# The root of a head's variance: from eleven VectorE steps to one GpSimd power instruction, for six of eight groups

## The chip, the cores and the metric

The kernel runs on one core of a Trainium2 chip. The metric is device time in microseconds (us). The kernel before takes 2485.27 us, the median of three runs (2484.48 to 2485.36). Smaller is better.

## The reference, cut to what matters

The kernel computes a two-layer decoder trunk on 256 tokens of width 2048, in float32. Layer 0 is an RWKV-7 time mix, layer 1 a block attention, and each is followed by a SwiGLU feed-forward part. The change touches one line of layer 0: the output `y` of the recurrence is normalised per token and per head of 64 columns.

```
y = _rwkv7_scan(rh, decay, kh, vh, -kk, kk * ah)        # 32 heads of 64
mu  = jnp.mean(y, axis=-1, keepdims=True)
var = jnp.mean(jnp.square(y - mu), axis=-1, keepdims=True)
yn  = ((y - mu) * lax.rsqrt(var + GN_EPS)).reshape(B, S, C) * lnx_w + lnx_b
bonus = (jnp.sum(rh * kh * r_k, axis=-1, keepdims=True) * vh).reshape(B, S, C)
return ((yn + bonus) * g) @ w_o
```

What is at issue is the factor `rsqrt(var + GN_EPS)`: 256 tokens by 32 heads, thus 8192 numbers in all.

## The kernel before, in words

All large weight products go through one scheme. SP loads a chunk of weights, ScalarE rounds it (`whi`, L1246), VectorE takes the rest (`wlo`, L1684), and TensorE does three products for each tile (L595 to L597). The recurrence lies between the projections and the output product, from about 280 to 520 us of the span.

The recurrence works on 8 groups (`GROUPS`) of 256 columns, four heads each, in 8 slots (`for s in range(GROUPS)`), one after another. Each engine has its own list of instructions in a written-out order, and semaphores join them. In slot `s` TensorE solves a triangular system for group `s` in five levels. `inner(s, l)` (L775) is a product whose result VectorE masks (L1846); `outer(s, l)` (L785) is a product whose result VectorE transposes (L1852, L1854) and ScalarE copies (L1368). Between these steps TensorE does the solution and the state of group `s - 1`, and `fill(n)` (L892, L882): pieces of a projection and of the gate, which are put there as filler. After `inner(s, 4)` TensorE runs `transposes_of(s + 1)` (L724 to L728). It waits there on `nat_done`, which GpSimd gives.

VectorE also does the normalisation of group `i = s - 2` in slot `s`, as parts of `group_norm`. Parts 0 and 1 (sum, mean and centring, L1887 to L1890) lie at the end of slot `s - 1`, then ScalarE squares (L1390). In slot `s`, part 2 (sum of squares L1893, scale and epsilon L1894) stands after `inner(s, 1)`, part 3 after `inner(s, 4)`, part 4 after `outer(s, 4)`, and part 5 (the product with the root, L1902) at the slot's end. Parts 3 and 4 are the root: two seed instructions (L1663, L1664) and three Newton steps of three (L1668 to L1670), each on 128 x 8 numbers, each waiting for the one before it. The last two groups, 6 and 7, are normalised after or at the end of the slots.

GpSimd's order in its loop over `g` from 1 to 7 is: for `g` 5 and 6 first `finish(g - 5)` and `load_w(g - 3)`; then `naturals(g)`, then `bonus(g - 2)` and `load_b(g)`. `naturals(g)` waits on `decay_done`, which ScalarE gives (L1301) in slot `g - 1`, and does five products on 128 x 512 (L507 to L511); the last gives `nat_done`. `finish(g)` multiplies the normalised group by its weight, adds the bonus and multiplies by the gate (L536 to L538); it waits on `y_normed`, which L1902 gives. `wait_aside` is a 128 x 1 instruction (L459) that carries a wait. At the start GpSimd clears `idle` (L452), waits for it, and issues three loads (L461 to L463).

Of the kernel before, what the change touches and what calls it, by code (L numbers as in the profile page):

```python
# [25 lines left out]
ALU = mybir.AluOpType  # L26
# [23 lines left out]
HD = 64  # L50
CHUNK = 64
PAIRS = D // P
GROUPS = PAIRS // 2
# [26 lines left out]
GN_EPS = 64e-5  # L80
# [74 lines left out]
def trunk(nc, x, rows, rwkv_rows, lora, w, consts, ln_rows, y):  # L155
    with ExitStack() as ctx:
        def sem(name):
            return ctx.enter_context(nc.semaphore(name))
# [10 lines left out]
        gsm = sb("gsm", [P, 5, 8])  # L169
# [4 lines left out]
        pad_ring = sb("pad_ring", [P, 176])  # L174
# [24 lines left out]
        def carve(base, at, *shape):  # L199
            n = int(np.prod(shape))  # L200
            v = base[:, at:at + n]
            if len(shape) == 1:
                return v
            names = "abcd"[:len(shape)]
            return v.rearrange(f"p ({' '.join(names)}) -> p {' '.join(names)}", **{q: n for q, n in zip(names[:-1], shape[:-1])})
# [36 lines left out]
        def mask(at, *shape):  # L242
# [11 lines left out]
        MQ = tmp("a2t", 2, 3, P)  # L254
        S = tmp("a2t", 2, 3, CHUNK)
        PC = carve(pad_ring, 0, 3, 2, 4)
        y_sq = carve(big, 32 * KB, TT, 2 * P)
        parb, parw = carve(a2t, 28 * KB, 2, 2 * P), carve(a2t, 30 * KB, 2, 2 * P)
        g2p = [tmp("rec2", 2, 2 * P) for _ in range(3)]
# [45 lines left out]
        ix_set, iz_made, iz_set, ixt_made, ixt_set, first_set, moved = (  # L305
            sem(n) for n in ("ix_set", "iz_made", "iz_set", "ixt_made", "ixt_set", "first_set", "moved"))
        y_centred, y_squared = sem("y_centred"), sem("y_squared")
        names = ("tr_made arT_set bkT_set g_made g_set av_made av_set uhw_made uhw_set "
                 "post_made s_made s_set y_made y_set")
        lq = [{n: sem(f"lane{s}_{n}") for n in names.split()} for s in range(2)]  # L310
# [139 lines left out]
        def _(pool):  # L450
            xv = x[0].rearrange("(t p) d -> p t d", p=P)
            nc.gpsimd.memset(idle[:], 0.0).then_inc(idle_set, 1)  # L452
            pool.wait_ge(idle_set, 1)

            def wait_aside(k, ready, value):

# [34 lines left out]
            def load_w(g):  # L491
                if g >= 2:
                    pool.wait_ge(zz_done, g - 1)
                load_row(parw, 3, g, parw_in)
# [7 lines left out]
            def naturals(g):  # L502

                cs = slice(g * 2 * P, (g + 1) * 2 * P)
                Pi, Pn, Pe = E[:, 0], E[:, 1], L_[:, :, cs]
                pool.wait_ge(decay_done, g + 1)
                then(5, nc.gpsimd.tensor_tensor(Pe, Pe, Pi, ALU.mult))  # L507
                nc.gpsimd.tensor_tensor(KN_[:, :, cs], KN_[:, :, cs], Pe, ALU.mult)
                nc.gpsimd.tensor_tensor(R_[:, :, cs], R_[:, :, cs], Pi, ALU.mult)
                for m in BH:  # L510
                    last = nc.gpsimd.tensor_tensor(m[:, :, cs], m[:, :, cs], Pn, ALU.mult)  # L511
                last.then_inc(nat_done, 1)
# [17 lines left out]
            def finish(g):  # L530

                yv, vv, gv = (m[:, :, g * 2 * P:(g + 1) * 2 * P] for m in (R_, KN_, L_))
                pool.wait_ge(parw_in[g % 2], 16 * (g // 2 + 1))
                wait_aside(3, gate_kept, g + 1)
                pool.wait_ge(y_normed, g + 1)
                then(4, nc.gpsimd.tensor_tensor(yv, yv, across(parw[:, g % 2]), ALU.mult))  # L536
                then(5, nc.gpsimd.tensor_tensor(yv, yv, vv, ALU.add))
                nc.gpsimd.tensor_tensor(yv, yv, gv, ALU.mult).then_inc(zz_done, 1)  # L538

            naturals(0)  # L540
            pool.wait_ge(chunk_used, PH["wo"][0])
            for g in range(2):
                load_b(g)
                load_w(g)
            for g in range(1, GROUPS):
                if g in (5, 6):
                    pool.wait_ge(y_normed, g - 3)
                    finish(g - 5)
                    load_w(g - 3)
                naturals(g)  # L550
                if g >= 2:
                    bonus(g - 2)
                    load_b(g)
            for g in range(2, 4):
                finish(g)
                load_w(g + 2)
            bonus(GROUPS - 2)
            for g in range(4, GROUPS - 2):
                finish(g)
# [672 lines left out]
        def _(act):  # L1232
# [54 lines left out]
            def decays(g):  # L1287
# [5 lines left out]
                ci = ps[:, 4].rearrange("p (t c) -> p t c", t=TT)  # L1293
                A(PC[:, g % 3].rearrange("p l c -> p (l c)"), ps[:, 6, 0:8], ACT.Exp)
                A(E[:, 0], ci, ACT.Exp)
# [355 lines left out]
        def _(dve):  # L1651
            V = nc.vector
            step = Count(dve_step)

            def then(ins):

                step.up(ins)
                dve.wait_ge(dve_step, step.now())
# [197 lines left out]
            def transitions(g, a):  # L1856
# [4 lines left out]
                V.tensor_tensor(MQ[:, a, 2, 0:CHUNK], ps[:, 5 + 2 * a, 3 * P:3 * P + CHUNK], ri[:, a, 3, 1], ALU.add)  # L1861
                V.tensor_scalar(S[:, a, 0], ps[:, 4 + 2 * a, P:P + CHUNK], PC[:, g % 3, a, 0:1], None, ALU.mult).then_inc(q["s_set"], 1)

            def state(g, c):

                at = P if c == 1 else P + CHUNK
                for a in (1, 0):
                    q = lq[a]
                    dve.wait_ge(q["s_made"], 2 * g + c)
                    V.tensor_scalar(S[:, a, c], ps[:, 4 + 2 * a + c % 2, at:at + CHUNK], PC[:, g % 3, a, c:c + 1], None,  # L1870
                                    ALU.mult).then_inc(q["s_set"], 1)

            def group_norm(i, part):

                cs = slice(i * 2 * P, (i + 1) * 2 * P)
                yv = R_[:, :, cs]

                def heads(v):
                    return v.rearrange("p t (h i) -> p t h i", i=HD)

                def per_head(v):
                    return v.rearrange("p (t h) -> p t h", t=TT).unsqueeze(3).broadcast_to([P, TT, 4, HD])

                if part == 0:
                    for q in lq:
                        dve.wait_ge(q["y_set"], i + 1)
                    then(V.tensor_reduce(gsm[:, 0].rearrange("p (t h) -> p t h", t=TT), heads(yv), AX.X, ALU.add))  # L1887
                    then(V.tensor_scalar(gsm[:, 1], gsm[:, 0], 1.0 / HD, None, ALU.mult))
                elif part == 1:
                    V.tensor_tensor(heads(yv), heads(yv), per_head(gsm[:, 1]), ALU.subtract).then_inc(y_centred, 1)  # L1890
                elif part == 2:
                    dve.wait_ge(y_squared, i + 1)
                    then(V.tensor_reduce(gsm[:, 0].rearrange("p (t h) -> p t h", t=TT), heads(y_sq), AX.X, ALU.add))  # L1893
                    then(V.tensor_scalar(gsm[:, 2], gsm[:, 0], 1.0 / HD, GN_EPS, ALU.mult, ALU.add))  # L1894
                elif part == 3:
                    rsqrt_seed(gsm[:, 3], gsm[:, 2], gsm[:, 4])
                    newton(gsm[:, 3], gsm[:, 2], gsm[:, 4])
                elif part == 4:
                    newton(gsm[:, 3], gsm[:, 2], gsm[:, 4])
                    newton(gsm[:, 3], gsm[:, 2], gsm[:, 4])  # L1900
                else:
                    V.tensor_tensor(heads(yv), heads(yv), per_head(gsm[:, 3]), ALU.mult).then_inc(y_normed, 1)  # L1902

            dve.wait_ge(chunk_used, PH["wo"][0])
# [9 lines left out]
            for s in range(GROUPS):  # L1914
                more = s + 1 < GROUPS

                def norm(part):
                    if s >= 2:
                        group_norm(s - 2, part)

                inner(s, 1)
                norm(2)
                outer(s, 1)
                inner(s, 2)
                if s:
                    transitions(s - 1, 1)
                    transitions(s - 1, 0)
                outer(s, 2)
                if s:
                    state(s - 1, 1)  # L1930
                inner(s, 3)
                if s:
                    state(s - 1, 2)
                outer(s, 3)
                inner(s, 4)
                norm(3)
                outer(s, 4)
                norm(4)
                if more:
                    masked_products(s + 1, 0)  # L1940
                inner(s, 5)
                if more:
                    first_block(s + 1, 0)
                    masked_products(s + 1, 1)
                    first_block(s + 1, 1)
                if s:
                    for part in range(2):
                        group_norm(s - 1, part)
                norm(5)
# [19 lines left out]
            def finish(g):  # L1969

                yv, vv, gv = (m[:, :, g * 2 * P:(g + 1) * 2 * P] for m in (R_, KN_, L_))
                dve.wait_ge(parw_in[g % 2], 16 * (g // 2 + 1))
                dve.wait_ge(gate_kept, g + 1)
                then(V.tensor_tensor(yv, yv, bcast_row(parw[:, g % 2]), ALU.mult))
                then(V.tensor_tensor(yv, yv, vv, ALU.add))
                V.tensor_tensor(yv, yv, gv, ALU.mult).then_inc(last_z, 1)
# [274 lines left out]
```

## Time and profile before

| | |
|---|---|
| median of 3 runs | 2485.27 us |
| lowest, highest | 2484.48, 2485.36 us |
| span of the profiled execution (first to last instruction) | 2481.7 us |
| time outside the span, against the median | 3.57 us |
| TensorE busy, instructions | 2444.9 us (99%), 15550 |
| VectorE busy | 1410.0 us (57%) |
| ScalarE busy | 1074.4 us (43%) |
| GpSimd busy | 126.0 us (5%) |
| mean granted TensorE clock | 0.998 |

The profiled execution has no time recorded for it beside its span of 2481.7 us, so the span stands for it; the 3.57 us are the difference to the median of the three timed runs. The profile names TensorE PE (its weight loads PEld), VectorE DVE, ScalarE ACT and GpSimd POOL. A row of the timeline gives the start, the time from the first start to the last end, engine, line, operation, output and input, shapes and the count of instructions merged in it. A bracket at its end gives the idle time before it and what ended that. A row of the waits gives who waited for whom, the total, the number of times and the longest. A busy TensorE is not necessarily at its peak, but here it leaves few gaps.

### The profile page before, as it was taken

How to read it: one execution, taken by the hardware profiler on the slowest of the kernel's cores; microseconds unless marked ns; L12 is line 12 of the kernel's file. 1: busy time of each engine (PE TensorE's matmuls, PEld its weight loads, DVE VectorE, ACT ScalarE, POOL GpSimd, SP SyncE). 2: the span in 40 equal slices, each digit the busy share in tenths (PEclk: the TensorE clock that was granted, in tenths of full speed). 3: DMA queues.
4: the chain of work that ended last, by engine and by line, in shares of the span. 5: the costliest groups of instructions: out<-in, count | busy, mean ns of one | idle time of the engine just before them, and what ended most of it. 6: DMA issues, size and time to landing. Idle time of an engine off the chain costs nothing.

```text
span 2481.7 us, 39434 instructions
## 1 busy us (share of the span) xinstructions
PE 2444.9 (99%) x15550; PEld 2003.2 (81%) x15550; DVE 1410.0 (57%) x1743; ACT 1074.4 (43%) x1347; POOL 126.0 (5%) x166
## 2 busy tenths in 40 slices
PE   8999999999999999999999999999999999999997
PEld 5888788877888888888887788888788888888886
DVE  6688566676744454454446544666745445454445
ACT  4454355444444444443334344453544444443332
POOL 1000235420000000000000000000000000000000
PEclk9999999999999999999999999999999999999999
DMA  7556411255666666665665565445566666666564
GB/s 233 179 195 205 136 42 38 66 208 188 196 192 188 186 193 186 188 188 193 193 195 198 195 193 188 143 167 190 170 187 192 188 186 193 186 194 221 189 194 143
DMA packets 225435, 440.87 MB, mean 178 GB/s; under 512 B 13472, under 2 KB 23744, under 8 KB 224224
## 3 DMA queue, kind: packets, MB, share of 16 engines
q1 hardware_dynamic: 221760, 417.38, 54.1%
q0 software_dynamic: 3552, 21.73, 2.6%
q8 instruction: 91, 1.49, 0.2%
q14 instruction: 32, 0.26, 0.0%
HBM read 436.96 MB, written 2.10 MB: 177 GB/s over the span
## 4 chain that ended last, share of the span: by engine, by line
PE 94%; DVE 3%; ACT 1%; issue 1%; DMA 1%; POOL 0%; DVEq 0%; ACTq 0%; SPq 0%; POOLq 0%
PE ps L595 25%; PE ps L597 25%; PE ps L596 25%; PE ps L892 3%; PE ps L1075 1%; PE ps L775 1%; PE ps L785 1%; PE ps L1103 1%; PE ps L622 1%; PE ps L624 1%; PE ps L623 1%; PE ps L882 1%; PE ps L836 1%; DVE wlo L1684 1%; PE ps L740 1%
## 5 line engine op out<-in xcount | busy, mean ns | idle before, releaser
L1246 ACT CAST whi<-raw 128x1024 fp32r<-128x1024 f32 x735 | 772.5, 1052 | 1145.9 <-PE ps L597 1080.1
L1684 DVE TENSOR_TENSOR wlo<-raw,whi 128x1024 fp32r<-128x1024 f32 x549 | 670.1, 1225 | 622.2 <-ACT whi L1246 620.3
L595 PE MATMUL ps<-whi,ahi 128*128 128x512 f32 x2172 | 851.5, 392 | 2.8 <-DVE wlo L1684 2.8
L597 PE MATMUL ps<-whi,alo 128*128 128x512 f32 x2172 | 845.6, 389 | 0.0
L596 PE MATMUL ps<-wlo,ahi 128*128 128x512 f32 x2172 | 845.1, 389 | 0.0
L595 PEld LDWEIGHTS ps<-whi,ahi 128*128 128x128 f32 x2172 | 407.8, 188 | 87.6 <-DVE wlo L1684 3.6
L597 PEld LDWEIGHTS ps<-whi,alo 128*128 128x128 f32 x2172 | 407.7, 188 | 85.5
L596 PEld LDWEIGHTS ps<-wlo,ahi 128*128 128x128 f32 x2172 | 407.9, 188 | 84.4 <-issue 1.0
L2015 DVE TENSOR_TENSOR wlo<-raw,whi 128x1024 fp32r<-128x1024 f32 x193 | 236.2, 1225 | 249.4 <-ACT whi L1246 247.4
L595 PE MATMUL ps<-whi,hThi 128*128 128x512 f32 x656 | 255.4, 389 | 0.0
L597 PE MATMUL ps<-whi,hTlo 128*128 128x512 f32 x656 | 255.2, 389 | 0.0
L596 PE MATMUL ps<-wlo,hThi 128*128 128x512 f32 x656 | 255.2, 389 | 0.0
L595 PEld LDWEIGHTS ps<-whi,hThi 128*128 128x128 f32 x656 | 123.1, 188 | 25.7
L596 PEld LDWEIGHTS ps<-wlo,hThi 128*128 128x128 f32 x656 | 123.1, 188 | 25.5
L597 PEld LDWEIGHTS ps<-whi,hTlo 128*128 128x128 f32 x656 | 123.1, 188 | 25.4
L892 PE MATMUL ps<-raw,big 128*128 128x256 f32 x256 | 67.7, 398 | 0.1
L571 POOL DMA_DIRECT2D big<-ln_rows x3 | 1.6, 537 | 1116.3 <-PE ps L624 787.1
L892 PEld LDWEIGHTS ps<-raw,big 128*128 128x128 f32 x256 | 44.8, 189 | 7.6 <-issue 0.3
L1516 ACT ACTIVATE a2t<-ps,lnT 128x128 f32<-128x128 f32 x96 | 34.2, 496 | 33.2 <-PE ps L1065 33.2
L1846 DVE TENSOR_TENSOR rec<-ps,big 128x512 f32<-128x512 f32 x40 | 27.6, 689 | 35.7 <-PE ps L775 35.7
L1693 DVE SCALAR_TENSOR_TENSOR big<-big,mixT 128x256 f32<-128x256 f32 x96 | 40.7, 479 | 0.5
L2118 DVE TENSOR_TENSOR hTlo<-ps,hThi 128x1024 f32 (+1 forms) x22 | 26.9, 1225 | 19.5 <-ACT hThi L1545 19.5
(317 smaller groups left out, 1933.8 us busy)
## 6 DMA issues: line engine op xcount, KB each, us to landing
raw<-w_up SPq DMA_DIRECT2D x176, 512.0 KB, 3.6
raw<-w_down SPq DMA_DIRECT2D x176, 512.0 KB, 4.0
raw<-w_gate SPq DMA_DIRECT2D x170, 512.0 KB, 3.6
raw<-w_k SPq DMA_DIRECT2D x32, 512.0 KB, 3.8
raw<-w_r SPq DMA_DIRECT2D x32, 512.0 KB, 4.4
raw<-w_v SPq DMA_DIRECT2D x32, 512.0 KB, 3.7
raw<-w_o SPq DMA_DIRECT2D x32, 512.0 KB, 4.8
raw<-kv_v SPq DMA_DIRECT2D x32, 512.0 KB, 3.7
```

The costliest lines, as they stand in the source:

```text
L595: mm(o, hi[:, k, tok], whi[:, s, k2, :], start=(k == 0), stop=False)
L596: mm(o, hi[:, k, tok], wlo[:, s, k2, :], start=False, stop=False)
L597: last = mm(o, lo[:, k, tok], whi[:, s, k2, :], start=False, stop=(k == kt - 1))
L622: mm(ps[:, 2 + t, :], hi[:, k, tok], wh[:, k2, :], start=False, stop=False)
L892: last = mm(ps[:, 3, t * T:(t + 1) * T], xxT[:, k, t * P:(t + 1) * P], rawf[:, s, k % FK], start=(i == 0), stop=(k == KT - 1), skip_group_ ...
L1246: nc.scalar.copy(whi[:, s], src).then_inc(hi_done, 1)
L1516: ins = A(hF[:, k, t * P:(t + 1) * P], ps[:, 4 + b, k2 * P:(k2 + 1) * P], ACT.Identity, scale=lnT[:, (n * 2) * KT + k:(n * 2) * KT + k + 1 ...
L1684: V.tensor_tensor(wlo[:, s], src, whi[:, s].bitcast(F32), ALU.subtract).then_inc(split_done, 1)
L1693: return V.scalar_tensor_tensor(out=out, in0=xxT[:, k], scalar=mixT[:, m * KT + k:m * KT + k + 1], in1=xT[:, k, 1:T + 1], op0=ALU.mult, op ...
L1846: V.tensor_tensor(Z.rearrange("p l (j c) -> p l j c", c=CHUNK), ps[:, 0:2, 0:4 * CHUNK].rearrange("p l (j c) -> p l j c", c=CHUNK), mask_l ...
L2015: V.tensor_tensor(wl, raw[:, s], wh.bitcast(F32), ALU.subtract).then_inc(split_done, 1)
L2118: V.tensor_tensor(hTlo[:, f0, :], ps[:, 4:6, :].rearrange("p a (k t) -> p (a k) t", k=2), hThi[:, f0, :].bitcast(F32), ALU.subtract).then_ ...
```

## The change

For groups 0 to 5 VectorE stops after part 2: L1894 signals `var_set`. GpSimd then runs `root(g)`, one `tensor_tensor` with the operation power, on 128 x 8 numbers, with a constant of minus one half as the other operand, and signals `root_set`. VectorE waits on it in part 5. Parts 3 and 4 disappear from the slots; groups 6 and 7 keep their eleven instructions. On GpSimd `root(g - 3)` stands first in the turn for `g` of 3 and more, ahead of `finish(g - 5)` and `naturals(g)`; `root(5)` stands between `finish(2)` with `load_w(4)`, and `finish(3)`. The constant is set at the start of the kernel, between the clearing of `idle` and the first loads.

```diff
+        minus_half = carve(pad_ring, 32, 8)
+        half_set, var_set, root_set = sem("half_set"), sem("var_set"), sem("root_set")
             nc.gpsimd.memset(idle[:], 0.0).then_inc(idle_set, 1)
             pool.wait_ge(idle_set, 1)
+            nc.gpsimd.memset(minus_half, -0.5).then_inc(half_set, 1)
...
+            def root(g):
+                pool.wait_ge(var_set, g + 1)
+                nc.gpsimd.tensor_tensor(gsm[:, 3], gsm[:, 2], minus_half, ALU.pow).then_inc(root_set, 1)
...
             naturals(0)
+            pool.wait_ge(half_set, 1)
...
             for g in range(1, GROUPS):
+                if g >= 3:
+                    root(g - 3)
                 if g in (5, 6):
                     pool.wait_ge(y_normed, g - 3)
                     finish(g - 5)
                     load_w(g - 3)
                 naturals(g)
...
-            for g in range(2, 4):
-                finish(g)
-                load_w(g + 2)
+            finish(2)
+            load_w(4)
+            root(GROUPS - 3)
+            finish(3)
+            load_w(5)
             bonus(GROUPS - 2)
...
-                    then(V.tensor_scalar(gsm[:, 2], gsm[:, 0], 1.0 / HD, GN_EPS, ALU.mult, ALU.add))
+                    ins = V.tensor_scalar(gsm[:, 2], gsm[:, 0], 1.0 / HD, GN_EPS, ALU.mult, ALU.add)
+                    if i < GROUPS - 2:
+                        ins.then_inc(var_set, 1)
+                    else:
+                        then(ins)
...
                 else:
+                    if i < GROUPS - 2:
+                        dve.wait_ge(root_set, i + 1)
                     V.tensor_tensor(heads(yv), heads(yv), per_head(gsm[:, 3]), ALU.mult).then_inc(y_normed, 1)
...
                 outer(s, 3)
                 inner(s, 4)
-                norm(3)
                 outer(s, 4)
-                norm(4)
```

## Rows read from the trace of the kernel before

**Rows 1.** The page's line of busy time by engine.
```profile
PE 2444.9 (99%) x15550; PEld 2003.2 (81%) x15550; DVE 1410.0 (57%) x1743; ACT 1074.4 (43%) x1347; POOL 126.0 (5%) x166
```

**Rows 2.** TensorE's waits on other engines, 340 to 504 us.
```profile
PE ps L775 <- DVE rec L1854: 0.5, 2, 0.2
PE ps L785 <- DVE rec L1846: 0.4, 1, 0.4
```

**Rows 3.** Groups of VectorE instructions, 345 to 504 us (busy us, mean ns, idle).
```profile
L1669 DVE SCALAR_TENSOR_TENSOR gsm<-gsm 128x8 f32<-128x8 f32 x18 | 3.0, 167 | 0.6
L1670 DVE SCALAR_TENSOR_TENSOR gsm<-gsm 128x8 f32<-128x8 f32 x18 | 3.0, 167 | 0.6
L1663 DVE TENSOR_SCALAR gsm<-gsm 128x8 int32<-128x8 int32 x6 | 2.8, 459 | 0.0
L1668 DVE TENSOR_TENSOR gsm<-gsm 128x8 f32<-128x8 f32 x18 | 2.7, 152 | 0.4
```

**Rows 4.** VectorE's timeline, what follows the two parts, slots 3 and 7.
```profile
387.82 0.45 DVE L1852 STREAM_TRANSPOSE rec<-ps 128x256 f32<-128x256 f32 x1 [1.01 <-PE ps L785]
...
389.91 1.35 DVE L1826 COPY_PREDICATED rec<-big,ps 128x512 f32<-128x512 uint32 x2 [0.26 <-PE ps L740]
...
497.85 0.45 DVE L1852 STREAM_TRANSPOSE rec<-ps 128x256 f32<-128x256 f32 x1
```

**Rows 5.** VectorE's timeline round the variance of slots 3, 4 and 5.
```profile
373.65 0.17 DVE L1894 TENSOR_SCALAR gsm<-gsm 128x8 f32<-128x8 f32 x1
...
396.81 0.69 DVE L1902 TENSOR_TENSOR big<-big,gsm 128x512 f32<-128x512 f32 x1
...
399.63 0.92 DVE L1894 TENSOR_SCALAR gsm<-gsm 128x8 f32<-128x8 f32 x1
400.58 0.45 DVE L1852 STREAM_TRANSPOSE rec<-ps 128x256 f32<-128x256 f32 x1
...
425.37 0.90 DVE L1894 TENSOR_SCALAR gsm<-gsm 128x8 f32<-128x8 f32 x1
```

**Rows 6.** GpSimd's timeline, finish and naturals, slots 4 and 5.
```profile
397.59 0.19 POOL L459 TENSOR_TENSOR idle<-idle 128x1 f32<-128x1 f32 x1 [10.74 <-DVE big L1902]
...
399.24 1.28 POOL L537 TENSOR_TENSOR big<-big 128x512 f32<-128x512 f32 x1
...
406.88 2.50 POOL L511 TENSOR_TENSOR big<-big 128x512 f32<-128x512 f32 x2
...
423.32 0.19 POOL L459 TENSOR_TENSOR idle<-idle 128x1 f32<-128x1 f32 x1 [10.41 <-DVE big L1902]
...
432.61 2.50 POOL L511 TENSOR_TENSOR big<-big 128x512 f32<-128x512 f32 x2
```

**Rows 7.** TensorE's timeline: the stall of slot 4, first transposes of slots 4, 5.
```profile
401.42 0.69 PE L775 MATMUL ps<-rec 64*64 64x64 f32 x32 [0.25 <-DVE rec L1854]
...
410.85 0.30 PE L724 MATMUL ps<-ident,big 128*128 128x128 f32 x1
...
437.19 0.33 PE L724 MATMUL ps<-ident,big 128*128 128x128 f32 x1
```

**Rows 8.** Slot 2 in the timelines of VectorE, GpSimd and TensorE.
```profile
347.97 0.17 DVE L1894 TENSOR_SCALAR gsm<-gsm 128x8 f32<-128x8 f32 x1
...
351.20 1.27 POOL L507 TENSOR_TENSOR big<-big 128x512 f32<-128x512 f32 x1 [16.59 <-ACT big L1301]
...
355.16 2.50 POOL L511 TENSOR_TENSOR big<-big 128x512 f32<-128x512 f32 x2
...
358.70 0.30 PE L724 MATMUL ps<-ident,big 128*128 128x128 f32 x1
```

**Rows 9.** GpSimd's timeline in slot 7: where finish(3) starts, and a later wait.
```profile
484.62 0.21 POOL L459 TENSOR_TENSOR idle<-idle 128x1 f32<-128x1 f32 x1
...
502.74 1.27 POOL L536 TENSOR_TENSOR big<-big,a2t 128x512 f32<-128x512 f32 x1 [4.65 <-DVE big L1902]
```

**Rows 10.** GpSimd's timeline at the start.
```profile
1.28 0.67 POOL L461 DMA_DIRECT2D ident<-consts  x1 [0.43 <-POOL idle L452]
```

## The prediction

> **What bounds the kernel now.** I read the page's busy line first: TensorE is busy 2444.9 of 2481.7 us, 99% [rows 1]. The span can shrink only where TensorE stands still, and it grows by whatever new wait TensorE gets. So the second view is TensorE's waits in the slots in which the removed instructions lie. There it waited 0.5 + 0.4 = 0.9 us for VectorE, in three places [rows 2]. The third view is VectorE's timeline: what comes right behind the removed parts, and did VectorE have to wait for it anyway? The fourth is GpSimd's timeline beside TensorE's, for the slack of the transposes that wait on `nat_done`.
>
> **What is removed.** In six slots eleven VectorE instructions go: 3.0 + 3.0 + 2.8 + 2.7 = 11.5 us of busy time [rows 3], and L1664, six times, which at the 0.17 us of its neighbours makes 1.0: 12.5 us. What are they worth? In slot 3, after part 3 VectorE idled 1.01 us until TensorE's `outer` was there, and after part 4 another 0.26 us until the products were there [rows 4]. Without the parts it idles longer, and TensorE gets its operands at the same time. In slot 7 the transpose L1852 at 497.85 has no idle before it [rows 4], so VectorE may be the later one; but TensorE's waits in the whole stretch are those of rows 2, and none of them is behind that transpose. I cost the removal at zero. What hides it is TensorE's own work (`outer`, filler, products). The bound of a gain is the 0.9 us that TensorE waited for VectorE.
>
> One part of these 0.9 us does go, by the moved order. The variance instruction L1894 took 0.17 us in slot 3, but 0.92 and 0.90 us in slots 4 and 5 [rows 5]. In slot 4 it ran from 399.63 to 400.55, and GpSimd's L537 ran from 399.24 to 400.52 [rows 6]: it ended with it. TensorE then waited 0.25 us for the transpose behind it [rows 7], and the same in slot 5, the 0.5 us of rows 2. With the change `finish` can't start before `var_set`, so L1894 runs in 0.17 us.
>
> The Trainium skill, page "SBUF — State Buffer", section "SBUF: two separate sides", says that VectorE and GpSimd share a pair of ports by an exclusive lock held for a whole instruction, and that the loser blocks fully. The two ends in slot 4, 0.03 us apart, agree with it. By that rule alone the power instruction would be a new blocker on VectorE. What follows L1894 is the transpose L1852 from PSUM, which took 0.45 us in slot 4 beside GpSimd's work and 0.45 us in slot 3 without it [rows 4, 5], so the rule changes no term of the sum.
>
> **What is added: `root` ahead of `finish`, slots 4 and 5.** This is the term that matters. For `g` of 5 and 6 GpSimd did `finish(g - 5)` as soon as L1902 at the end of the last slot was done, at 397.59 and 423.32 [rows 6]. Now `root` comes first, and waits for L1894 of the current slot. Let R be the time of the power instruction.
> - Slot 4: L1894 ends at 399.63 + 0.17 = 399.80. From a VectorE end to a GpSimd start I take 0.09 us, from the end of L1902, 396.81 + 0.69 = 397.50 [rows 5], to 397.59 [rows 6]. Consecutive GpSimd instructions overlap by some 0.04 us. So `finish` starts at 399.80 + 0.09 - 0.04 + R = 399.85 + R, later by 2.26 + R. `naturals(5)` follows it directly, as before, and ended at 406.88 + 2.50 = 409.38. It ends at 411.64 + R. TensorE's first transpose was at 410.85 [rows 7], a slack of 1.47 us. With 0.09 us of signal, TensorE starts it at 411.73 + R: a new wait that costs 0.88 + R. The 0.25 us gained above are in this: TensorE comes earlier and waits longer.
> - Slot 5: L1894 ends at 425.37 + 0.17 = 425.54, `finish` starts at 425.59 + R, later by 2.27 + R. `naturals(6)` ended at 432.61 + 2.50 = 435.11, the transposes began at 437.19: slack 2.08. Cost 2.27 + 0.09 - 2.08 + R = 0.28 + R, on top of the first, since everything in this slot is shifted alike.
>
> Sum of both: 1.16 + 2R.
>
> TensorE runs in order, so its filler behind the transposes can't be drawn ahead, and later stages have too few waits to take the loss back.
>
> **R.** No row of the trace shows a power instruction. From below: a 128 x 1 product took 0.19 us [rows 6], so R is at least about 0.2. A 128 x 512 sum (L537) took 1.28 us, so a column costs (1.28 - 0.19) / 511 = 2.1 ns. A power is a logarithm and an exponential, computed on GpSimd in many operations. I take forty for each of 8 columns: 8 x 40 x 2.1 ns = 0.7 us and 0.19 around it, R = 0.9 us; forty is an estimate. From above: if each of the 8 columns cost as much as a whole 128 x 512 product, R would be 8 x 1.28 = 10.2 us. Between ends so far apart I stay near the small one, since the instruction has 8 columns and the 128 x 1 row is the nearest in size; the range keeps more.
>
> **Other slots.** In slots 2, 3 and 6 `root` stands ahead of `naturals` alone, which waits for ScalarE. In slot 2, the tightest, L1894 ends at 348.14, `root` can start at 348.23, and `naturals` began at 351.20 [rows 8]: 2.97 us of cover. It ended at 357.66 and the transposes began at 358.70, another 1.04 - 0.09 = 0.95 us. R is hidden up to 3.9 us. If it were longer, TensorE would wait here too. In slot 7 `root(5)` comes after 484.62 at the earliest and pushes `finish(3)`, the bonus and `finish(4)` by R; GpSimd later waits 4.65 us there for VectorE [rows 9], which takes it up. Behind the new wait in part 5 VectorE's next slot is queued, and all of TensorE waits for that. But L1902 comes 23 us after L1894 (373.82 to 396.81, [rows 5]), and in slot 7 it ends 18 us after the root can start (484.62 to 502.67): nothing.
>
> **Start.** One more memset stands before GpSimd's three loads, the last of which TensorE's first instruction waits for. Between the memset of `idle` and the first load 0.43 us passed, mostly the wait for it [rows 10]. The new one is issued in that stretch's tail; I take 0.05 us, with bounds of 0 and 0.43 (a second stretch of the kind).
>
> **Sum.** 1.16 + 2 x 0.9 + 0.05 = 3.0 us. On the span 2481.7 + 3.0 = 2484.7; nothing that lies around the span (3.57 us against the median) changes, so on the median 2485.27 + 3.0 = 2488.3 us, slower by 0.12%. About 0.2%, 5.0 us, is what a measurement of this kernel can tell from no change; so this is a forecast of "within 0.2%".
>
> **Rivals.**
> - *The power instruction is long, and GpSimd becomes the late one.* The mechanism is the one above: each microsecond of R counts twice, in slots 4 and 5. For: software, and no row. Against: only 8 columns. It decides from R = 1.9 us (1.16 + 3.8 = 5.0). With R = 4 it gives 1.16 + 8 = 9.2, 2494.5 us; with R = 10, slot 2 adds 6.1, slot 3 a similar amount (I take 5) and the sum is 32, 2518 us. Chance 0.22.
> - *VectorE's queue is worth more than TensorE's waits show,* because TensorE's busy time hides stalls. At the most, 12.5 us of busy time come back, 2473 us. Against: VectorE idles after both parts in slot 3, and TensorE's filler runs back to back. Half of it would be 2480. Chance 0.05.
> - *The wait for `nat_done` does not bite:* the slack of the transposes is larger than the timeline shows, or later stages give the shift back (TensorE waits for VectorE and ScalarE there too). Then the 0.9 us of rows 2 are all there is to gain, 2484.4 to 2485.5 us. For: the slack in slot 5 is short by 0.28 + R only. Chance 0.13.
> - The forecast, R from 0.2 to 1.9 us: 2486.5 to 2490.3 us. Chance 0.60.
>
> **How the numbers follow.** Faster by over 0.2% is the second rival alone, 0.05. Slower by over 0.2% is the first, 0.22, and 0.01 of the forecast's upper edge, thus 0.23. Within 0.2%: 0.59 + 0.13 = 0.72. The range goes from 2484.9 (into the third rival) to 2493.5 (R = 3.5, so into the first); what lies outside is about 0.05 below from the second rival, 0.05 from the third, and 0.09 above.
>
> The Trainium skill, page "GPSIMD Engine Reference", section "4.1 Engine selection", puts elementwise work on VectorE and calls GpSimd about twice as slow for two inputs. In this trace a 128 x 512 product takes 0.69 us on VectorE [rows 5] and 1.27 us on GpSimd [rows 8], which agrees; by it alone the eleven small instructions would be better left where VectorE has slack.
>
> **What would show it.** Right: L1894 at 0.17 us in slots 4 and 5; GpSimd's `finish(0)` starting some 2.3 us + R later; TensorE with new waits for GpSimd's L511 ahead of L724, twice, 1.8 and 1.2 us; VectorE idle longer before L1852 and L1826; TensorE's busy time the same; the power instruction near 0.9 us. Wrong: a power instruction of several microseconds; no wait before L724; or slots that are shorter although TensorE did not wait for VectorE in them.

## The result, and the profile after

| | before | after |
|---|---|---|
| median of 8 runs each | 2486.72 us (2484.48 to 2489.98) | 2491.73 us (2490.39 to 2494.09) |
| ratio | | 1.0023, 95% interval 1.0014 to 1.0031 |
| span of the profiled execution | 2481.7 us | 2488.8 us |

The change makes the kernel slower by 5.0 us in the medians, 5.7 us by the ratio. Measured a second time, with other runs of both, it was 1.0028 (1.0019 to 1.0037). The forecast was 2488.3 us, 3.0 us slower, in a range of 2484.9 to 2493.5. Of the 3.4 us between 2488.3 and 2491.73, 1.45 are the base: over eight runs the kernel before has 2486.72 us, not the 2485.27 of three.

The page of the kernel after, the line of busy time by engine, answers to [rows 1]:

```profile
PE 2446.8 (98%) x15550; PEld 2004.9 (81%) x15550; DVE 1397.3 (56%) x1677; ACT 1074.1 (43%) x1347; POOL 136.3 (5%) x173
```

VectorE lost 66 instructions and 12.7 us, GpSimd gained 7 instructions and 10.3 us. TensorE has the same instructions. Its waits in the recurrence, 340 to 530 us of the kernel after, answer to [rows 2] (who waited for whom, total, times, longest):

```profile
PE ps L737 <- POOL big L514: 4.6, 2, 2.4
PE ps L849 <- issue: 1.7, 2, 1.1
PE ps L875 <- issue: 1.4, 2, 1.1
PE ps L798 <- DVE rec L1859: 0.3, 1, 0.3
```

L737 and L514 are L724 and L511 of before: the transposes wait for the last product of `naturals`. The two short waits for a transpose of VectorE are gone. The timeline of GpSimd after, slots 4 and 5, answers to [rows 6]; L546 is the power:

```profile
401.03 1.67 POOL L546 TENSOR_TENSOR gsm<-gsm,pad_ring 128x8 f32<-128x8 f32 x1 [13.56 <-DVE gsm L1907]
402.68 0.18 POOL L462 TENSOR_TENSOR idle<-idle 128x1 f32<-128x1 f32 x1
...
412.01 2.47 POOL L514 TENSOR_TENSOR big<-big 128x512 f32<-128x512 f32 x2
...
429.34 1.67 POOL L546 TENSOR_TENSOR gsm<-gsm,pad_ring 128x8 f32<-128x8 f32 x1 [11.32 <-DVE gsm L1907]
...
440.32 2.48 POOL L514 TENSOR_TENSOR big<-big 128x512 f32<-128x512 f32 x2
```

`finish(0)` starts at 402.68 instead of 397.59, and the last product ends at 414.48 instead of 409.38. Of these 5.1 us, 1.14 lie ahead of slot 4's variance instruction (400.77 instead of 399.63); the rest, 3.95 us, answers to the 2.26 + R of the prediction, 3.93 at R = 1.67. TensorE's timeline after answers to [rows 7], and VectorE's variance instruction (L1907, L1894 of before) to [rows 5]:

```profile
414.54 0.33 PE L737 MATMUL ps<-ident,big 128*128 128x128 f32 x1 [2.43 <-POOL big L514]
...
442.86 0.33 PE L737 MATMUL ps<-ident,big 128*128 128x128 f32 x1 [2.20 <-POOL big L514]
...
443.93 0.42 PE L737 MATMUL ps<-ident,big 128*128 128x128 f32 x1
```
```profile
400.77 0.17 DVE L1907 TENSOR_SCALAR gsm<-gsm 128x8 f32<-128x8 f32 x1
```

The third TensorE row is new in kind: the same transpose takes 0.42 us and not 0.27. The stretches of the kernel after say why (busy time by engine, then the granted clock, DMA share and rate):

```profile
442.00:443.00 1.00, 0.14 (x1) 0.14 (x2) 0.00 (x0) 0.00 (x0) 1.00 (x3) 1.00 0.11 28
443.00:444.00 1.00, 1.00 (x9) 1.00 (x9) 0.00 (x0) 0.00 (x0) 0.95 (x1) 0.82 0.02 7
444.00:445.00 1.00, 1.00 (x7) 1.00 (x6) 0.00 (x0) 0.83 (x2) 0.97 (x2) 0.50 0.00 0
445.00:446.00 1.00, 1.00 (x12) 0.67 (x15) 0.00 (x0) 0.25 (x1) 0.70 (x2) 0.50 0.00 0
446.00:447.00 1.00, 1.00 (x33) 0.88 (x29) 0.03 (x1) 0.03 (x1) 0.34 (x1) 0.50 0.00 0
```

Some 0.8 us behind the end of the wait the granted clock fell to 0.50 (1.2 GHz of 2.4), for 3.4 us. What that cost is read from VectorE's masks of level 4 and level 5 in slot 5, before and after:

```profile
437.32 0.69 DVE L1846 TENSOR_TENSOR rec<-ps,big 128x512 f32<-128x512 f32 x1 [1.73 <-PE ps L775]
...
443.24 0.68 DVE L1846 TENSOR_TENSOR rec<-ps,big 128x512 f32<-128x512 f32 x1
```
```profile
440.72 0.69 DVE L1859 TENSOR_TENSOR rec<-ps,big 128x512 f32<-128x512 f32 x1 [1.73 <-PE ps L788]
...
450.40 0.68 DVE L1859 TENSOR_TENSOR rec<-ps,big 128x512 f32<-128x512 f32 x1
```

They were 5.92 us apart before, and 9.68 us after. Of these 3.76 us more, 2.20 are the wait; the other 1.56 are put down to the slow clock.

So the 7.1 us between the two spans are made up of: waits for GpSimd 2.43 + 2.20 = 4.63, slow clock 1.56, less the waits for VectorE that went (0.25 + 0.23 + 0.07 = 0.55), together 5.6; and TensorE's stalls without a releaser (idle time for which the profile shows no cause, its "issue") between 320 and 410 us, 2.60 us before (1.35, 0.49, 0.76) and 4.14 after (1.07, 1.12, 0.32, 1.05, 0.58), 1.5 us more. The last item is the doubtful one, and the first experiment is for it.

### The profile page after: what moved, and what is told of

It reads as the page before. It is cut to its first block, busy times and chain, and to the rows that moved or that the text cites. A ratio compares the mean times of both kernels' runs of the same rounds, so it can differ in the third digit from the quotient of the medians.

```text
span 2488.8 us, 39358 instructions
## 1 busy us (share of the span) xinstructions
PE 2446.8 (98%) x15550; PEld 2004.9 (81%) x15550; DVE 1397.3 (56%) x1677; ACT 1074.1 (43%) x1347; POOL 136.3 (5%) x173
## 4 chain that ended last, share of the span: by engine, by line
PE 92%; DVE 3%; issue 2%; POOL 2%; ACT 1%; DMA 1%; DVEq 0%; POOLq 0%; ACTq 0%; SPq 0%
PE ps L608 25%; PE ps L610 25%; PE ps L609 25%; PE ps L905 2%; PE ps L1088 1%; PE ps L1116 1%; PE ps L637 1%; PE ps L636 1%; PE ps L635 1%; PE ps L895 1%; PE ps L798 1%; DVE wlo L1697 1%; PE ps L788 1%; PE ps L932 1%; PE ps L690 1%
```

## The experiments

Theory A: the loss comes from GpSimd's order alone (the power ahead of `finish`, with its length), and from the clock that falls behind TensorE's waits. Each was timed against the kernel before on the same chip.

**The kernel before again, and the changed kernel again.** No edit.

> The kernel before, unchanged, as a kernel of its own: shows how far two runs of the same program lie apart. Theory A (the loss is GpSimd's order and the length of the power, 1.67 us, plus a fall of TensorE's clock): ratio 1.000 +- 0.001, no TensorE wait for GpSimd's last product of naturals, clock 1.00 from 340 to 500 us, stalls of TensorE without a releaser between 320 and 410 us of 2 to 4 us in total, as they would be a matter of the run and not of the change. Rival B (those stalls grew from 2.6 us to 4.1 us because of the change): 2.6 us again.

> The changed kernel, unchanged. Theory A: slower by 5 to 7 us, two waits of 2.2 to 2.5 us before the transposes of slots 4 and 5, and after the second a stretch of some 3 us at half the granted clock again, if the fall follows from the waits. Rival B (the fall of the clock was a chance of one execution): 1.00 throughout, and slower by 4.5 us. Stalls without releaser: A 2 to 4 us, B 4.1 us.

Measured: 1.0000 (0.9991 to 1.0009) and 1.0028 (1.0019 to 1.0037). The second trace of the kernel before has 3.8 us of stalls without a releaser between 320 and 410 us (1.21, 1.03, 0.75, 0.58, 0.22), and its span is 2482.3. So most of the 1.5 us is there without the change. The second trace of the changed kernel has 5.0 us of them (1.36, 0.77, 0.38, 1.32, 1.13), more than either side expected; the executions differ too much in them for a difference of 1 us to mean anything. The second trace of the changed kernel, TensorE's waits from 340 to 530 us and a late stretch:

```profile
PE ps L739 <- POOL big L516: 3.9, 2, 2.0
```
```profile
1380.00:1385.00 5.00, 3.02 (x12) 2.17 (x12) 2.98 (x3) 2.58 (x3) 0.00 (x0) 1.00 0.32 105
1385.00:1390.00 5.00, 4.31 (x12) 3.42 (x13) 4.04 (x4) 2.21 (x3) 0.00 (x0) 0.66 0.52 178
```

The waits are 1.89 and 2.02 us, and the clock did not fall behind them. It fell at 1385 instead, behind a wait of 2.43 us for VectorE at the end of layer 0 which the kernel before has too (2.42 us, without a fall). Both sides were partly wrong: the fall is real and can come at any wait of this size, but not in every execution.

One execution can't say how much the clock costs on average, but the record has the mean granted clock and the span of every one. The eleven of the changed kernel average 0.9966 and 2491.0 us, the 33 of the kernel before 0.9978 and 2483.9 us. An estimate from these: 0.0012 of 2491 us is 3.0 us of work at full clock, so about two falls in an execution, each 3.4 us at half and thus 1.7 us of such work. Waits of 3.9 us, less the 0.55, and 3.0 us make 6.4 of the 7.1 us between the spans. The clocks are on record to three places only.

**The root behind `naturals`.**

```diff
             for g in range(1, GROUPS):
-                if g >= 3:
-                    root(g - 3)
...
                 naturals(g)
+                if g >= 3:
+                    root(g - 3)
```

> The changed kernel with one edit: in GpSimd's loop root(g - 3) stands behind naturals(g), not at the head of the turn. The root then comes some 10 us before it is used. Theory A (all loss comes from the place of the root ahead of finish): no wait before the transposes, clock 1.00, time 0 +- 1 us against before; the variance instruction at 0.9 us in slots 4 and 5 again. Rival C (the power instruction or the wait for it costs by itself, by the shared ports or on VectorE): still slower by 2 us or more. Rival D (VectorE's removed work is worth something): faster by 1 us or more.

Measured: 1.0001 (0.9992 to 1.0010), 2486.5 us. No wait of TensorE for GpSimd, clock 1.00. The six powers took 1.66 to 1.67 us each, as in the changed kernel, and cost nothing that can be measured. The loss is the place of the instruction; of rivals C and D there is no sign, but the interval, 2.0 us faster to 2.5 us slower, leaves room for effects of 1 to 2 us. One thing more stands in this trace: the variance instruction took 0.90 us in slots 4 and 5, and TensorE still had no wait of 0.2 us for VectorE there. The change also took away VectorE's own wait behind that instruction: in slot 4 the transpose now started 0.09 us ahead of its end (401.61 and 401.70), and 0.03 us behind it in the kernel before. So the collision is only a part of the two waits of 0.25 us.

**`finish` behind `naturals`.**

```diff
                 if g >= 3:
                     root(g - 3)
+                naturals(g)
                 if g in (5, 6):
...
                     load_w(g - 3)
-                naturals(g)
```

> The changed kernel with the root at the head of the turn as it is, and finish(g - 5) with its load behind naturals(g) for g of 5 and 6. Theory A: no wait before the transposes and no collision of the variance instruction (0.17 us in every slot), so TensorE's two waits of 0.25 us go as well: faster than before by 0 to 0.5 us, and by 5 to 7 us than the changed kernel. Rival C: slower than before by 2 us or more. Rival: the late finish collides with VectorE's masks at the slot's end and costs some 1 us.

Measured: 0.9998 (0.9989 to 1.0007), 2485.52 us. The variance instruction took 0.17 us in all slots, and TensorE's waits for GpSimd and for the transposes are gone. The interval goes from 2.7 us faster to 1.7 us slower, so whether the 0.5 us expected back came can't be told. TensorE's waits of this kernel, 340 to 530 us:

```profile
PE ps L849 <- issue: 1.6, 2, 0.8
PE ps L788 <- issue: 1.4, 1, 1.4
PE ps L875 <- issue: 0.8, 1, 0.8
PE ps L798 <- DVE rec L1859: 0.3, 1, 0.3
```

The stalls without a releaser are 1.6 + 1.4 + 0.8 = 3.8 us here, against 1.3 and 2.5 us in the two traces of the kernel before, which differ by more than 0.5 us between themselves. This version has the lowest ratio of those timed, and it isn't measurably faster than the kernel before.

**The removal alone.** `norm(3)` and `norm(4)` are taken out of the slots of the kernel before.

```diff
-                norm(3)
                 outer(s, 4)
-                norm(4)
...
-                    V.tensor_tensor(heads(yv), heads(yv), per_head(gsm[:, 3]), ALU.mult).then_inc(y_normed, 1)
+                    V.tensor_tensor(heads(yv), heads(yv), per_head(gsm[:, 3 if i >= GROUPS - 2 else 2]), ALU.mult).then_inc(y_normed, 1)
```

> The kernel before without parts 3 and 4 in the slots (66 VectorE instructions), GpSimd untouched; groups 0 to 5 are multiplied by the variance itself, so their root is left out of the computation. Theory A: VectorE's removed work lay beside TensorE's, time 0 +- 1 us. Rival D (it was worth something that TensorE's waits do not show): faster by 3 to 12 us.

Measured: 1.0000 (0.9991 to 1.0009). Taking 66 VectorE instructions away is worth nothing that can be measured, that is, less than some 2.2 us; the 3 us or more of rival D are excluded.

**The steps kept.** The changed kernel, with `norm(3)` and `norm(4)` back, into a row that is not read.

```diff
+                to = 3 if i >= GROUPS - 2 else 1
...              (parts 3 and 4 write gsm[:, to] in the place of gsm[:, 3])
                 inner(s, 4)
+                norm(3)
                 outer(s, 4)
+                norm(4)
```

> The changed kernel, with the eleven VectorE instructions put back in their places for groups 0 to 5, writing a row that nobody reads. Theory A: same as the changed kernel, slower than before by 5 to 7 us, since only GpSimd's order counts. Rival D: slower still, by the value of the removed work (3 us or more above the changed kernel).

Measured: 1.0029 (1.0018 to 1.0040), the same as the changed kernel's 1.0028. One wait appeared in the trace. VectorE's and GpSimd's timelines of this kernel, slot 7:

```profile
503.73 1.11 DVE L1676 TENSOR_SCALAR gsm<-gsm 128x8 int32<-128x8 int32 x1
504.87 0.17 DVE L1677 TENSOR_SCALAR gsm<-gsm 128x8 int32<-128x8 int32 x1
505.07 1.26 DVE L1681 TENSOR_TENSOR gsm<-gsm 128x8 f32<-128x8 f32 x1
```
```profile
503.53 1.27 POOL L540 TENSOR_TENSOR big<-big 128x512 f32<-128x512 f32 x1
...
505.05 1.26 POOL L541 TENSOR_TENSOR big<-big 128x512 f32<-128x512 f32 x1
```

The late `finish` now runs beside the Newton steps, two of which last until GpSimd's product is done, and TensorE waits 0.93 us for VectorE. In the changed kernel those steps are gone, and its trace has no such wait. So with the new order the removal saves this one wait in the trace; the timed runs don't show it. By the Trainium skill, page "SBUF — State Buffer", section "SBUF: two separate sides", GpSimd and a VectorE instruction with two SBUF inputs (or in one of its 2-port modes) exclude each other: whichever starts first keeps the shared ports for its whole instruction, and the other is blocked. L1681 has two SBUF inputs, starts 0.02 us behind GpSimd's L541 and ends 0.02 us behind it, which agrees; L1676 ends 0.04 us behind L540, and that it ran in a 2-port mode no row shows.

**A product for the power; the power twice.**

```diff
-                nc.gpsimd.tensor_tensor(gsm[:, 3], gsm[:, 2], minus_half, ALU.pow).then_inc(root_set, 1)
+                nc.gpsimd.tensor_tensor(gsm[:, 3], gsm[:, 2], minus_half, ALU.mult).then_inc(root_set, 1)
```
```diff
+        extra = carve(pad_ring, 48, 8)
...
+                nc.gpsimd.tensor_tensor(extra, gsm[:, 2], minus_half, ALU.pow)
                 nc.gpsimd.tensor_tensor(gsm[:, 3], gsm[:, 2], minus_half, ALU.pow).then_inc(root_set, 1)
```

> The changed kernel with a product in the place of the power, same operands and waits; the root of groups 0 to 5 is thus left out of the computation. Theory A with R of about 0.2 us: waits of 0.9 + 0.2 = 1.1 and 0.3 + 0.2 = 0.5 us before the transposes, 1.2 + 2 x 0.2 = 1.6 us slower than before, no fall of the clock. Rival B (the loss is the order alone, whatever the instruction takes): slower by 5 us as the changed kernel.

> The changed kernel with a second power of the same shape, into a row that nobody reads, right ahead of each root: R = 3.3 us. Theory A: waits of 4.2 and 3.6 us before the transposes, and with two falls of the clock at about 1.5 us each some 10 to 11 us slower than before. Slots 2, 3 and 6 still hide it (3.3 us is under 3.9). Rival: the clock falls for longer or costs nothing: 13 us or more, or 7.8 us.

Measured: 1.0004 (0.9995 to 1.0014) and 1.0047 (1.0033 to 1.0061). TensorE's waits for GpSimd in the two, 340 to 530 us:

```profile
PE ps L737 <- POOL big L514: 1.1, 2, 0.7
```
```profile
PE ps L739 <- POOL big L515: 7.7, 2, 4.0
```

With R of 0.20, 1.67 and 3.30 us the two waits sum to 1.1, 3.9 to 4.6 and 7.7 us: 2.1 us for each microsecond of R, which is the 2R of the sum. The product is slower than before by 1.0 us, at most 3.5, so the 5 us of rival B are excluded: the length of the instruction counts too. Twice the power is slower by 11.7 us (8.2 to 15.2), a little above the 10 to 11 expected. It let the clock fall in both slots (0.68 in 416 to 424, 0.79 in 448 to 456); in slot 4 the fall began some 2 us ahead of the wait's end and lasted 6.8 us.

Why do the waits of slot 4 differ at the same R, 1.89 to 2.59 us? Between that slot's variance instruction and its transposes, at about 404 us, lies one of TensorE's stalls without a releaser, and what it takes is missing from the wait. TensorE's stall and wait in slot 4 of the kernel after:

```profile
404.39 0.27 PE L849 MATMUL ps<-a2t 64*64 64x64 f32 x1 [0.58 <-issue]
...
414.54 0.33 PE L737 MATMUL ps<-ident,big 128*128 128x128 f32 x1 [2.43 <-POOL big L514]
```

Their sum is 0.58 + 2.43 = 3.01 us here, 1.13 + 1.89 = 3.02 in its second trace, 0.42 + 2.59 = 3.01 with the steps kept and 0.43 + 2.58 = 3.01 with the root first in slot 4 only (below). With the product, 1.47 us shorter, it is 1.14 + 0.34 = 1.48.

**The root first in one slot only.** In the one kernel the root stands behind `naturals` in slot 5, in the other in slot 4 (the comments in the cut give the other kernel's values).

```diff
-                if g >= 3:
+                if g in (3, 4, 5, 7):          # other kernel: (3, 4, 6, 7)
                     root(g - 3)
...
                 naturals(g)
+                if g == 6:                     # other kernel: 5
+                    root(g - 3)
```

> The changed kernel, with the root at the head of GpSimd's turn in slots 2, 3, 4 and 6 and behind naturals in slot 5. Theory A: one wait of 0.88 + 1.67 = 2.5 us before the transposes of slot 4, none in slot 5. If the clock falls only after the second stretch of idle time: clock 1.00 and 2.3 us slower than before. Rival: one idle stretch is enough, the clock falls behind it, and it costs 1.5 us more.

> The mirror of the other: the root at the head of the turn in slots 2, 3, 5 and 6 and behind naturals in slot 4. Theory A: one wait of 0.28 + 1.67 = 1.95 us (2.2 measured with both) before the transposes of slot 5, none in slot 4. If the fall needs the earlier stretch too: clock 1.00, 1.7 us slower than before. Rival (it is slot 5's own place that lets the clock fall): the clock falls here as in the changed kernel, 3.5 us slower.

Measured: 1.0009 (1.0000 to 1.0018) and 1.0011 (1.0002 to 1.0020), so 2 to 3 us each by the medians, and 0 to 5 us by the intervals. In both profiled executions the clock fell, as the rivals said. The stretch behind the one wait, slot 4 in the first kernel, and slot 5 in the second:

```profile
413.00:420.00 7.00, 6.06 (x86) 5.43 (x90) 0.85 (x2) 2.79 (x7) 4.04 (x6) 0.76 0.10 21
```
```profile
439.00:446.00 7.00, 6.11 (x88) 5.28 (x92) 0.85 (x2) 2.80 (x7) 3.99 (x6) 0.76 0.13 24
```

The waits were 2.58 and 2.19 us. One wait can be enough, then, but it isn't always. In the first kernel the profiled execution is the slowest of eleven (2491.33 us, median 2488.73); the eleven have a mean clock of 0.9980 against 0.9977 for the 21 executions of the kernel before timed beside them, and their mean span is 2.2 us longer, which is the wait without a fall. In the second kernel it is 0.9975 and 3.0 us. So the time of the first fits Theory A (2.3 us) better than its rival (3.8), and the second lies between A (1.7 us) and its rival (3.5 us).

**The power by its size.** Powers and products one by one, on GpSimd at the end of the kernel before's recurrence.

```diff
+            for op, n in ((ALU.pow, 1), (ALU.pow, 4), (ALU.pow, 8), (ALU.pow, 16), (ALU.pow, 32), (ALU.mult, 8), (ALU.mult, 32)):
+                then(8, nc.gpsimd.tensor_tensor(out[:, 0:n], two[:, 0:n], half_neg[:, 0:n], op))
```

> The kernel before with powers of 128 x 1, 4, 8, 16 and 32 and products of 128 x 8 and 32, one by one, on GpSimd in its idle stretch after the recurrence, values 2.0 and -0.5. Theory A (software, one column after another): 1.67 us at 8, straight in the number of columns: about 0.35 us at 1 and 6 us at 32, if the fixed part is that of a product (0.2 us); the product about 0.2 us at 8 and 0.25 at 32. Rival (a fixed cost of over 1 us): 1.2 us or more at 1 column.

GpSimd's timeline of this kernel:

```profile
522.54 0.58 POOL L569 TENSOR_TENSOR pad_ring<-pad_ring 128x1 f32<-128x1 f32 x1
...
523.34 1.02 POOL L569 TENSOR_TENSOR pad_ring<-pad_ring 128x4 f32<-128x4 f32 x1
...
525.22 1.63 POOL L569 TENSOR_TENSOR pad_ring<-pad_ring 128x8 f32<-128x8 f32 x1
...
527.08 2.90 POOL L569 TENSOR_TENSOR pad_ring<-pad_ring 128x16 f32<-128x16 f32 x1
...
530.35 5.89 POOL L569 TENSOR_TENSOR pad_ring<-pad_ring 128x32 f32<-128x32 f32 x1
```

From 1 to 32 columns it is (5.89 - 0.58) / 31 = 0.17 us a column, 0.15 between the small sizes and 0.19 between 16 and 32, and some 0.4 us besides. The fixed part is thus above the 0.2 us expected, and one column cost 0.58 us and not 0.35; the rival's 1.2 us is excluded. The products took 0.20 us at 8 columns and 0.25 at 32. A product costs 0.0021 us a column [rows 6, 8], so a column of power costs eighty times as much.

## Why the prediction was right where it was, and where not

- **The removal costs and brings nothing: right, as far as it can be measured.** Removal alone gave 1.0000, give or take 2.2 us. Slot 7's transpose with no idle time before it [rows 4] was no bound either: before its next mask VectorE now idles 1.27 us and not 0.16.
- **The collision of L1894 goes: right** (0.92 to 0.17 us), and with it the 0.5 us of waits. In the changed kernel these were swallowed by the longer wait, as the prediction said. Its account of them was not whole: with the collision back (root behind `naturals`) they stayed away, because VectorE no longer waits for its own L1894.
- **The order is the term that matters, 1.16 + 2R: right in place and in form.** At the measured R of 1.67 it gives 4.5 us; the traces show 4.6 and 3.9. By slots it gives 2.55 and 1.95, and 2.43 and 2.20 were measured. With a product in the power's place it gives 1.6, and 1.1 was measured. What it left out is the stall at 404 us, which the trace that it was read from doesn't have, and which took up to 1.1 us of the wait in slot 4.
- **R of 0.9 us: the mis-sized term.** It measured 1.67 us. "Forty for each of 8 columns" should have been about eighty. Two times 0.77 are 1.5 us of the difference. This term alone would have made it 2489.8 us.
- **The clock: not in the prediction.** The sum took a wait of TensorE at its own length. Of the seven waits for GpSimd of 2.19 us and more, six came with half the clock; the one whose cost was read cost 1.56 us. 4.5 + 0.05 + 1.56 = 6.1 us is in the interval of both measurements of the change (3.5 to 7.7 and 4.7 to 9.2 us); 4.55 us without the clock is in the first alone. The mean clocks put the term nearer to 3 us.
- **The start: right.** The first load began at 1.31 instead of 1.28 us, 0.03 us later.
- **Other slots: right.** In slots 2, 3 and 6 TensorE never waited for GpSimd, even with 3.3 us of powers (cover 3.9).
- **The rivals.** "The power is long" decides from 1.9 us, and R is 1.67: it did not hold by its own bound, but the time went to the bound of 0.2% with the clock's help (0.23%, interval 0.14 to 0.31). VectorE's queue was worth nothing that can be measured. The wait for `nat_done` did bite.
- **The range held by its width.** Its upper part was meant for a power of up to 3.5 us. What filled it was a power of 1.67 us, a clock that the sum has no term for, and a base 1.45 us higher; that the sum of these stayed below 2493.5 is in part luck.

What stays open: what TensorE's stalls without a releaser are. They lie among the small products, mostly those of the state, near 326, 351, 379 and 404 us, and sum to 2.6 to 5 us from 320 to 410 us, with and without the change. Whether they take up small gains elsewhere is not shown; no kernel here was made to test them. Open too is why the clock falls at some waits of this size and not at others, and what the fall costs on average other than by the estimate from the mean clocks.

## What to carry to other kernels

When work is moved to an engine with time to spare, its busy share is not the question, but what stands behind the moved instruction in that engine's queue and who waits for that: here 1.67 us of work on an engine busy 5% of the time held up TensorE twice, through two unrelated jobs. Place such an instruction behind the one with a deadline, if its own result is needed late; the same power instruction then cost nothing measurable. And count what a removed instruction covered: eleven instructions a slot beside a busy TensorE were worth nothing measurable.

## What the runs showed of the hardware

- GpSimd's power took 0.58 us for 128 x 1 and 5.89 us for 128 x 32, 0.17 us a column; a product of 128 x 8 took 0.20 us.
- TensorE's granted clock fell to 0.50 at a wait for GpSimd of 2.19 us (root first in slot 5 only), 2.20 (the kernel after), 2.58 (first in slot 4 only), 2.59 (steps kept), 3.71 and 4.01 (power twice), for 3.4 us each, at 4.01 for 6.8 us. It didn't at 2.43 (the kernel after), nor at 0.34 to 2.02. The fall began between 2 us ahead of the wait's end and 0.8 us behind it. At the wait of 2.4 us for VectorE at the end of layer 0, which the kernels have with and without the change, it fell in 3 of 13 profiled executions; all three are among the seven in which TensorE had waited for GpSimd before, which are too few to tell whether that matters.
- A small VectorE instruction on SBUF data took up to 1.27 us beside a GpSimd product (kernel after, L1677 at 511.39), and 0.17 us without; the transposes from PSUM took 0.45 us either way.
